# The opening of the even layer in an encoder trunk: tile loads, engine orders and turns rearranged

## What is computed

```python
def _trunk(x, pre_norm, post_norm, even_params, odd_params):
    for layer in range(DEPTH):
        h = _rms(x, pre_norm[layer])
        ...
            m = _even_mixer(h, *[p[j] for p in even_params])
        ...
        x = x + _rms(m, post_norm[layer])
    return x

def _even_mixer(h, w_in, ...):
    u_a, z_a, c_q, c_kv, k_rope, z_b = _split(h @ w_in, EVEN_SPLITS)
```

## Time and profile before

| | us |
|---|---|
| three runs: median (lowest to highest) | 3293.43 (3292.34 to 3297.87) |
| the profiled execution | 3296.31 |
| its span | 3294.7 |
| TensorE's matmuls busy | 3216.8 (98%) |
| VectorE busy | 1665.9 (51%) |
| ScalarE busy | 1419.3 (43%) |
| GpSimd busy | 633.7 (19%) |
| mean granted TensorE clock | 0.994 of full speed |

### The profile page before, as it was taken

How to read it: one execution, slowest core, us unless ns; L and a number is a source line. 1 busy time by engine, 2 the same in 40 slices (tenths; PEclk the granted TensorE clock), 3 DMA queues, 4 the chain that set the end, 5 groups by cost and what they waited for, 6 DMA issues and landing times. The chain is left out here.

```text
span 3294.7 us, 44203 instructions
## 1 busy us (share of the span) xinstructions
PE 3216.8 (98%) x16472; PEld 2672.8 (81%) x16472; DVE 1665.9 (51%) x3137; ACT 1419.3 (43%) x2568; POOL 633.7 (19%) x447
## 2 busy tenths in 40 slices
PE   7999999999899999999999999999999999999999
PEld 6877777878688888788788888888888888887887
DVE  4899999848666666511313233233322524666211
ACT  5233233143666666500325545455554325654100
POOL 4111111122411110032231010110112112331221
PEclk9999999999999999899999999999999999999999
DMA  4333333276412111643333232322322354445531
GB/s 132 90 93 96 91 98 104 80 219 219 124 46 57 41 46 40 187 116 107 118 90 107 88 120 77 123 82 79 114 79 90 124 184 140 135 148 178 167 100 54
DMA packets 414916, 360.79 MB, mean 110 GB/s; under 512 B 68472, under 2 KB 350584, under 8 KB 414704
## 3 DMA queue, kind: packets, MB, share of 16 engines
q1 hardware_dynamic: 329696, 264.35, 27.9%
q10 hardware_dynamic: 85008, 93.61, 8.1%
HBM read 231.01 MB, written 126.86 MB: 109 GB/s over the span
## 5 line engine op out<-in xcount | busy, mean ns | idle before, releaser
L2850 ACT ACTIVATE eow_w1raw<-of_ring 128x512 f32<-128x512 f32 x218 | 126.5, 595 | 397.7 <-PE of_ring L3251 395.0
L900 PE MATMUL ef_ring<-ef_hhi,ef_whi 128*128 128x512 f32 x720 | 288.9, 401 | 2.0 <-issue 1.0
L902 PE MATMUL ef_ring<-ef_hhi,ef_wlo 128*128 128x512 f32 x720 | 281.4, 391 | 0.0
L901 PE MATMUL ef_ring<-ef_hlo,ef_whi 128*128 128x512 f32 x720 | 281.4, 391 | 0.0
L3077 DVE SCALAR_TENSOR_TENSOR of_state<-of_state,of_small,of_tv 128x256 f32<-128x256 f32 x64 | 56.1, 877 | 242.2 <-ACT of_tv L2912 240.1
L900 PEld LDWEIGHTS ef_ring<-ef_hhi,ef_whi 128*128 128x128 f32 x720 | 135.5, 188 | 41.9 <-issue 14.9
L520 ACT ACTIVATE ef_stage<-ef_ring 128x512 f32<-128x512 f32 x90 | 53.4, 594 | 252.8 <-PE ef_ring L902 252.7
L902 PEld LDWEIGHTS ef_ring<-ef_hhi,ef_wlo 128*128 128x128 f32 x720 | 135.4, 188 | 29.6
L901 PEld LDWEIGHTS ef_ring<-ef_hlo,ef_whi 128*128 128x128 f32 x720 | 135.7, 188 | 26.2
L2767 POOL TENSOR_TENSOR eo_w0lo<-of_wraw,eo_w0hi 128x1024 fp32r<-128x1024 f32 x27 | 66.6, 2466 | 453.4 <-ACT eo_w0hi L2804 453.4
L2767 POOL TENSOR_TENSOR eo_whi<-of_wraw,eo_whi 128x1024 fp32r<-128x1024 f32 x26 | 64.7, 2490 | 434.2 <-ACT eo_whi L2804 434.2
(11 more groups left out here) (670 smaller groups left out, 9311.6 us busy)
## 6 DMA issues: line engine op xcount, KB each, us to landing
of_wraw<-o_w_in SPq DMA_DIRECT2D x53, 512.0 KB, 3.9
ef_wraw<-e_w_in SPq DMA_DIRECT2D x29, 512.0 KB, 4.1
s_tmo<-eow_w1raw ACTq DMA_DIRECT2D x48, 256.0 KB, 2.3
ow_raw<-s_yt SPq DMA_DIRECT2D x18, 512.0 KB, 5.7
ow_raw<-o_w_out SPq DMA_DIRECT2D x16, 512.0 KB, 5.0
s_uc<-ef_stage ACTq DMA_DIRECT2D x24, 256.0 KB, 2.5
ef_ut<-s_uc SPq DMA_DIRECT2D x16, 384.0 KB, 3.9
s_za<-ef_stage ACTq DMA_DIRECT2D x24, 256.0 KB, 2.0
```

What stands on the lines that cost most here:

```text
L900: pe.matmul(out, ah, hhi[:, f, tc], start=(f == 0), stop=False)
L901: pe.matmul(out, ah, hlo[:, f, tc], start=False, stop=False)
L902: mm = pe.matmul(out, al, hhi[:, f, tc], start=False, stop=(f == KT - 1))
L2850: act.activation(stage[i % 4][:, :], ring[i % 3][:, :] if i else start.first, func, scale=GK ** -0.5 if name == "q" else 1.0).then_inc(eva ...
```

## The change

- SyncE loads token tiles 0 to 3 first, then weight tile 0, then tiles 4 to 7, then weight tile 1. The two constants are issued by ScalarE.
- ScalarE takes square and root of tiles 0 to 3 one after the other, then high halves, weight tile 0 and squares in a list written out up to tile 7. From tile 8 on its loop is `square(i)`, `root(i)`, `h_hi(i-2)`.
- VectorE has weight tile 0's low half behind scale 3 and ahead of gains 2 and 3; from tile 4 on its loop is `mean(i)`, `scale(i)` and, from 6 on, `gains(i-2)`.
- GpSimd makes weight tile 1's low half ahead of token tile 4 instead of tile 5.
- TensorE has four turns, the first half of group 0 (12 of its 24 matmuls), turns 4 and 5, its second half, turns 6 and 7, the first half of group 1, turns 8 and 9, its second half, turn 10, the first half of group 2, turn 11, its second half.

No computation is added or taken away; the numbers of instructions are the same.

```diff
--- before.py
+++ after.py
@@ -353,15 +353,12 @@
                         sp.dma_start(wt[t * GC:(t + 1) * GC, :, :],
                                      d["lagrow"][4 * b:4 * b + 4, :, at:at + TC].rearrange("g c n -> c g n")).then_inc(wt_in, 16)
 
+                for i in range(4):
+                    x_load(i)
                 w_load(0)
-                x_load(0)
-                sp.dma_start(ident[:, :], d["ident"][:, :]).then_inc(const_in, 16)
-                sp.dma_start(gcol[:, :], d["pre_col"][0]).then_inc(const_in, 16)
-                for i in range(1, 6):
+                for i in range(4, 8):
                     x_load(i)
                 w_load(1)
-                for i in range(6, 8):
-                    x_load(i)
                 for k, name in enumerate(("lam_re", "lam_im", "log_dt")):
                     sp.dma_start(small[:, k, :].rearrange("p (a b) -> p a b", a=2), d[name]).then_inc(s5_in, 16)
                 for a in range(4):
@@ -418,7 +415,7 @@
 
                 pool.memset(warm[:, :], 1.0).then_inc(warm_set, 1)
                 for i in range(NT):
-                    if i == 5:
+                    if i == 4:
                         w_lo(1)
                     pool.wait_ge(hi_done, i + 1)
                     pool.tensor_tensor(hlo[:, :, i * P:(i + 1) * P], hf[i % 2].rearrange("p (k t) -> p k t", k=KT),
@@ -528,24 +525,39 @@
                     for to, dr, at in ((slice(0, 8), 1, slice(0, TC)), (slice(8, 15), 0, slice(GC, TC))):
                         act.activation(rows[:, to, :].rearrange("p l c -> p (l c)"), pk[64 * dr:64 * dr + 64, at], ACT.Copy).then_inc(row_copy, 1)
 
+                act.dma_start(ident[:, :], d["ident"][:, :]).then_inc(const_in, 16)
+                act.dma_start(gcol[:, :], d["pre_col"][0]).then_inc(const_in, 16)
                 act.wait_ge(warm_set, 1)
                 act.activation(warm[:, 1:2], warm[:, 0:1], ACT.Sqrt).then_inc(warm_done, 1)
+                for i in range(4):
+                    square(i)
+                    root(i)
+                h_hi(0)
                 w_hi(0)
-                act.wait_ge(const_in, 32)
-                square(0)
-                for i in range(NT + 2):
-                    if i + 1 < NT:
-                        square(i + 1)
-                    if i < NT:
-                        root(i)
-                    if i == 6:
-                        w_hi(1)
-                    if i >= 2:
-                        h_hi(i - 2)
+                h_hi(1)
+                h_hi(2)
+                square(4)
+                h_hi(3)
+                root(4)
+                square(5)
+                root(5)
+                square(6)
+                root(6)
+                w_hi(1)
+                square(7)
+                root(7)
+                h_hi(4)
+                h_hi(5)
+                for i in range(8, NT):
+                    square(i)
+                    root(i)
+                    h_hi(i - 2)
                     if i == 9:
                         evac(("g", 0))
                     if i == 11:
                         evac(("g", 1))
+                h_hi(NT - 2)
+                h_hi(NT - 1)
                 done = 2
 
                 def catch_up(n, done):
@@ -633,17 +645,28 @@
                                           tp[i % 2][:, h * 512:(h + 1) * 512].rearrange("p (k t) -> p k t", k=4),
                                           bc(gcol[:, 4 * h:4 * h + 4], 2, P), ALU.mult).then_inc(hf_done, 1)
 
+                mean(0)
+                scale(0)
+                mean(1)
+                scale(1)
+                dve.wait_ge(const_in, 32)
+                gains(0)
+                mean(2)
+                scale(2)
+                mean(3)
+                gains(1)
+                scale(3)
                 dve.wait_ge(whi_done, 1)
                 tt(grouped(wlo[0][:, :, :]), by_group(wraw[:, :, :]), grouped(whi[0][:, :, :]).bitcast(F32), ALU.subtract).then_inc(wlo_done, 1)
-                dve.wait_ge(const_in, 32)
-                mean(0)
-                for i in range(NT + 1):
-                    if i + 1 < NT:
-                        mean(i + 1)
-                    if i < NT:
-                        scale(i)
-                    if i >= 1:
-                        gains(i - 1)
+                gains(2)
+                gains(3)
+                for i in range(4, NT):
+                    mean(i)
+                    scale(i)
+                    if i >= 6:
+                        gains(i - 2)
+                gains(NT - 2)
+                gains(NT - 1)
 
                 def sm(k):
                     return keep[:, :] if k == 15 else small[:, k, :]
@@ -887,20 +910,22 @@
                         mm = pe.transpose(tp[i % 2][:, k * P:(k + 1) * P], xt[i % 4][:, k * P:(k + 1) * P], ident[:, :])
                     mm.then_inc(tp_done, 1)
 
-                def group(n):
+                def group(n, part=(0, KT)):
                     k, c = order[n]
-                    pe.wait_ge(wlo_done, k + 1)
-                    pe.wait_ge(lo_done, 4 * (c + 1))
-                    if n >= 3:
-                        pe.wait_ge(evac_done, place[("g", n - 3)] + 1)
+                    if part[0] == 0:
+                        pe.wait_ge(wlo_done, k + 1)
+                        pe.wait_ge(lo_done, 4 * (c + 1))
+                        if n >= 3:
+                            pe.wait_ge(evac_done, place[("g", n - 3)] + 1)
                     tc = slice(c * 512, (c + 1) * 512)
                     out = ring[n % 3][:, :]
-                    for f in range(KT):
+                    for f in range(*part):
                         ah, al = whi[k % 2][:, f, :], wlo[k % 2][:, f, :]
                         pe.matmul(out, ah, hhi[:, f, tc], start=(f == 0), stop=False)
                         pe.matmul(out, ah, hlo[:, f, tc], start=False, stop=False)
                         mm = pe.matmul(out, al, hhi[:, f, tc], start=False, stop=(f == KT - 1))
-                    mm.then_inc(grp_done, 1)
+                    if part[1] == KT:
+                        mm.then_inc(grp_done, 1)
 
                 def bt_flip(b):
                     for j in range(2):
@@ -966,17 +991,22 @@
                                         mm.then_inc(y_mm, 1)
 
                 pe.wait_ge(const_in, 32)
-                for i in range(6):
+                for i in range(4):
                     flip(i)
-                group(0)
+                group(0, (0, KT // 2))
+                flip(4)
+                flip(5)
+                group(0, (KT // 2, KT))
                 flip(6)
                 flip(7)
-                group(1)
+                group(1, (0, KT // 2))
                 flip(8)
                 flip(9)
-                group(2)
+                group(1, (KT // 2, KT))
                 flip(10)
+                group(2, (0, KT // 2))
                 flip(11)
+                group(2, (KT // 2, KT))
                 for n in range(3, LEAD):
                     group(n)
                 lag(0)
```

## The result

| | before | changed |
|---|---|---|
| median of ten runs (lowest to highest), us | 3295.64 (3292.34 to 3300.09) | 3305.31 (3301.28 to 3313.26) |
| ratio of the changed kernel to the one before | | 1.0031, 95% interval 1.0022 to 1.0039 |
| the profiled execution: time, span | 3296.31, 3294.7 | 3313.26, 3311.7 |
| start of group 0, of group 4 | 28.24, 58.65 | 29.41, 70.01 |

The changed kernel is slower, by 10.2 us by the ratio (7.3 to 12.9), against a forecast of 11.0 us and a time of 3304.4.

What follows compares the result with a forecast made beforehand. Group 4's start was taken as the whole measure: 8.6 + 5.05 - 2.7 = 11.0 us later. The profiled 3296.3 became 3307.3, less 2.9 for the three-run median: 3304.4, range 3298.0 to 3308.5 (8 in 10).

Steps and rivals of the forecast that it cites:

- The measure: Opening: the start of group 4 on TensorE decides everything, 69.6 instead of 58.65, and nothing behind it absorbs the shift.
- three stretches: Shift of group 4: 8.6 to tile 5's high half, 5.05 more to tile 9's, 2.7 less to group 4.
- The loads: Start of the opening: tile 0 lands at about 6.5, first turn at about 9.1, 3.3 us earlier than before.
- The tie: VectorE's and GpSimd's low halves both want to start at 18.7; group 0 at 29.4, between 28.3 and 30.5.
- the case that was put at 30.5: Meeting at 18.7: GpSimd's low half of tile 1 starts before VectorE's weight low half, group 0 at 30.5.
- The clock: First half of group 0 on TensorE: all twelve matmuls at the lower clock, 5.1 us, done at 34.7.
- lower end: Lower bound of the time: scale 3 ahead of tile 0's low half and the old clock, 4.0 less, 3300.4.
- rival 2: Opening: one-tile ring but good start, group 0 at 26.6, old clock, no stretched scales; same, 3299.2; chance 0.12.
- rival 3: TensorE's clock stays at half level through the tile rounds, 2 to 3 us more, 3307; chance 0.10.
- The ring: Tiles 6 to 9: steps from square to high half no longer overlap between tiles, 5.3 us a round.
- rival 1: Opening: the head start holds if high halves 6 to 9 come every 3.5 us or faster; 3291.9; chance 0.03.
- The turns: TensorE: turns 4 and 5 follow half of group 0, at 34.5 and 35.4; within the 8.6 to tile 5's high half.

Runs made afterwards that it cites:

- e11: The changed kernel run again unaltered for a second trace; 3307.18 us, group 4 at 70.18.
- e7: The changed kernel with 56 unused turns of the identity on TensorE between turn 3 and group 0; 3306.2 us, group 4 at 67.92.
- e2: The changed kernel with square and mean one tile ahead again from tile 8 on, gains left in place; no time given, group 4 at 70.40.
- e1: The changed kernel with VectorE's gains i-2 ahead of mean i from tile 8 on; 3300.40 us, ratio 1.0010 to the kernel before.
- e9: The changed kernel with gains i-2 ahead of mean i from tile 8 and weight tile 0's low half behind gains 3; 3295.83 us, ratio 0.9999 to before.
- e6: The kernel before with only TensorE's changed order of turns and half groups; no time given, group 4 at 65.35.
- e4: The changed kernel with TensorE's old order of turns and whole groups; no time given, group 4 at 66.85.
- e10: The changed kernel's loads with the old turns and searched ScalarE and VectorE lists; 3292.34 us, ratio 0.9991 to the kernel before.

## Why the prediction was right, step by step

**The measure.** It said that group 4's start is the whole of it, at 69.6: measured 70.01. In the three stretches of its sum: the high half of tile 5 ended at 40.64 (said 40.4); from there to that of tile 9 21.2 us (21.2); from there to group 4 8.2 us (8.0). Nothing behind absorbed the shift: the last stage starts 10.9 us later in e11, where group 4 starts 11.5 later.

**The loads.** First turn at 8.65 (said 9.1). The scale of tile 3 started at 14.96 (15.9). Most of it is the first tile, whose square started at 5.94 where the load was put at 6.5; the squares of tiles 1 and 2 follow at 8.07 and 10.25, 1.07 to 1.09 us a half instead of 1.1. Everything up to here was 0.5 to 0.9 us early.

**The tie.** GpSimd was first, by 0.06 us, the case that was put at 30.5; since all was 0.9 earlier, it gave 29.41. The forecast's 29.4 was the middle between two cases, and is right partly by luck. The price of such a meeting, bounded by two rows, held: 2.87 for a scale (said 2.9), and for the subtraction 1.68 us behind the other's end (20.04 to 21.72), 0.2 less than its own 1.89. (The Trainium skill, "SBUF — State Buffer", section "SBUF: two separate sides", has the later of the two blocked for the whole of the other; the 3.97 us agree: 2.29 of waiting and 1.68 of work.)

**The clock.** Twelve slow matmuls, 5.25 us (said 5.1); e7 shows their worth at group 4, 2.1 us. That it was all twelve is luck in part: e11 and e2 have it too (5.26 and 5.19), e1 and e9 have 4.14 and 4.77. For its lower end and for rival 2 the forecast put the old kernel's first twelve matmuls at 3.9 us; they took 4.21 (28.24 to 32.45), so both come out 0.3 us too low. The fall of the clock behind the wait of 4.2 us came too (0.56 from 50 to 56). It made the second half of group 1 4.4 us long instead of 2.7 and turn 10 0.8 us late; turn 11 then still waited 0.81 us for gains 9, so it cost nothing: rival 3 had its mechanism and not its price. For the same reason the waits before turns 9, 10 and 11 were 4.20, none and 0.81 us where some 4, 2 and 2 were forecast.

**The ring.** 5.3 us a round, said 5.3, and the chain of steps is that of the forecast. Its last half microsecond was made a little otherwise: three of the four scales were stretched (tiles 8, 9 and 11: 1.35, 1.28 and 1.33 us) and the evacuation fell into the fourth, where two and one were assumed.

The forecast gave two links for it, that ScalarE runs square i+1 behind high half i-2 and that VectorE runs gains i-2 behind scale i. They are not two causes; a ring needs both. What counts is how many tiles it advances in one round, and that can be read from the lists. In the changed kernel high half i-3 leads to square i, mean i, scale i, gains i-2 and high half i-2: one tile in 5.3 us. In e2 it leads to square i+1, mean i+1, scale i, gains i-2 and high half i-2: still one tile. In e1, with gains ahead of the mean, it leads to square i, mean i, scale i, gains i-1 and high half i-1: two tiles in a round of about the same length, 5.6 us from high half 6 (41.49) to high half 8 (47.09), hence the 2.7 to 2.9 us a tile measured there. So of the two edits that were tried the one at the gains opens the ring, as rival 1's condition had it, and the one at the look-ahead does not.

**The turns.** The forecast put the late turns into its first stretch, 8.6 us of it, and did not price them by themselves. e6 and e4 do: 6.7 us alone in the old kernel, 3.2 in the changed one.

**The rivals.** Rival 1 (3291.9) came true only in another order: e10 reaches 56.1 at group 4, a little below that rival's 57.1. Rival 2 failed at its start: no part of the tie fell the way it needed.

## What to carry to other kernels

When several engines pass tiles from one to the next, follow one round through all their lists and count the tiles that it advances: if a step for tile i-2 (here the gains) stands behind a step of tile i whose input comes from behind the previous tile's last step, it advances one, and the round's whole latency is the time per tile, however idle every engine is. Move that one step ahead, so that the round advances two, before anything is loaded earlier. And a consumer that starts sooner gains nothing if the instructions that feed its successors are queued behind it.

## What the runs showed of the hardware that was not expected

Who starts first decides a meeting of VectorE and GpSimd, and here the difference was 0.06 us. GpSimd's low half started first, and VectorE's subtraction, 1.89 us when it met nothing, lasted 3.97. In e10 the same subtraction started 1.0 us ahead of a low half; it lasted 1.96, and the low half 3.14 instead of 2.37:

```profile
18.57 1.96 DVE L672 TENSOR_TENSOR ef_wlo<-ef_wraw,ef_whi 128x1024 fp32r<-128x1024 f32 x1 [0.19 <-ACT ef_whi L455]
...
19.57 3.14 POOL L421 TENSOR_TENSOR ef_hlo<-ef_area,ef_hhi 128x1024 fp32r<-128x1024 f32 x1 [1.73 <-ACT ef_hhi L469]
```

How many matmuls are slow at the start of group 0 differs with the work ahead of it, and also from one execution to the next. In the kernel before, with turns up to 0.4 us ahead of it, it was the first seven (until 31.30, 3.1 us). Behind 9.6 us of idle it was all twelve of the first half in the changed kernel, 5.25 us, and six in e1, behind the same wait. Behind 56 filler turns and 2.6 us of idle it was none.

The start of group 4 repeats to 0.2 us in two profiles of one kernel, in both pairs that there are. Most of the times' scatter therefore lies elsewhere: one late stage of one execution took 6 us more. But the first twelve matmuls, 1.1 us shorter in e1 than behind the same list and wait in the changed kernel, show that the opening has a share in it.
